# Layer 0's first norm: x projected un-normalized for three column blocks, then normalized in place by GpSimd

## The chip, the cores and the metric

One core of one Trainium2 chip. The metric is device time in microseconds (us) of one execution of the whole program, two layers of a hybrid model step. The engines are TensorE (PE), VectorE (DVE), ScalarE (ACT), GpSimd (POOL) and SyncE (SP, which here issues most DMAs).

## The reference, cut to what matters

The program runs 1024 prompt tokens and 32 sample tokens (8 sequences of 4) through two layers. What the change touches is how each layer begins:

```
def rmsnorm(x, g):                      # mean over the 1024 features of a token
    y = x * rsqrt(mean(x * x) + EPS)
    return y * g
h = rmsnorm(x, g_pre_mix[l])            # x: 1056 tokens x 1024
a_h, a_b, a_c, b_q, b_k, b_v, c_q, c_k, c_v, c_qi, c_ki, c_wi, d_u, d_v = split(h @ w_in[l])
# four mixers follow: a gated convolution, dilated attention, sparse attention with an
# indexer (c_qi, c_ki, c_wi) that picks 256 keys per query, and a gated spatial mix;
# then x += rmsnorm(m @ w_o), a feed-forward with its norms, and the next layer
```

Since `(x * r * g) @ W = r * (x @ (g * W))`, with `r` one number per token, the norm can be put before the projection, or its gain into the weights and its `r` behind the projection.

## The kernel before, in words

x lies transposed in SBUF, features on partitions: `xT` and `hT` are [128, 8, 1056] (8 chunks of 128 features, 1056 tokens). Tokens come in nine tiles of 128 (the last has the 32 sample tokens).

`load_x` is a block of its own, and a barrier of all engines ends it. SP loads the nine tiles of x as they are in HBM (512 KB each), then the gain `g`, the first two column blocks of `w_in` (`load_columns`), constants and the rope tables, and writes x to a parking place in HBM (`xpark`, three pieces). PE turns each tile with 8 transposes. DVE and ACT copy them out of PSUM into `xT`. ACT squares x, PE sums the squares over partitions with matmuls against ones, ACT takes the root, DVE inverts it and writes `hT`, the normalized x, for tokens 0 to 383. POOL starts 12 gathers of index pages.

`mix_in` projects. Its work is a list of units, each one token tile (or third) of one column block, in this order in layer 0: units 0 to 4 are block IX (the indexer's columns) of tiles 0 to 4; 5 to 7 are CV of tiles 0 to 2; 8 to 11 are IX of tiles 5 to 8; 12 to 17 are CV of the rest; 18 to 26 are CQ; 27 to 35 are CK; then DV, A0, A1, BQ, BK, BV, AB, DU. Two weight slots alternate by block. For each unit PE runs `project(i)`; ACT copies the result out (`unload`), DVE applies rope to the blocks that want it (`rotate`), and PE turns these four units later (`turn`), so unit 4 of PE stands behind the rope of unit 0, and unit 29 behind that of unit 25. All queues are written out by hand in unit order. A sample tile is projected in part beside the tile that `parts_at` names, and summed at the end of its block.

In layer 0 the rest of the norm is in `mix_in`: DVE's `second_norm` writes `hT` for tokens 384 to 767 before its first rope, and for the last 288 tokens ACT squares (`square_left`), PE sums (lines 876 and 881, at units 4 and 5), ACT takes the root, and DVE's `invert_left` and `norm_left` (lines 1352, 1358) write `hT` at unit 6. Layer 1 does the same for its last third, with a different source.

DVE waits ahead of its first rope for `in_`, six DMAs of constants, whose last is `own_col` (512 KB into `ext_p`), the first DMA that SP issues in `mix_in`. From unit 8 on, index scores are computed beside the projections (PE `index_heads`, ACT `index_relu`, DVE `index_scores`). At unit 24 DVE runs `search_begin`, which multiplies seven score tiles by a sign (line 1217) and then begins a bitwise search for each row's 256th score (line 1195 and the small operations of lines 1231, 1232, 1200) that goes on beside the projections to the end of `mix_in`.

The waits that matter: PE's `project` waits for `second_h` at unit 3 and for `left_h` from unit 8 on.

Of the kernel before, what the change touches and what calls it, by code (L numbers as in the profile page):

```python
# [6 lines left out]
ALU = mybir.AluOpType  # L7
# [8 lines left out]
P = 128  # L16
# [61 lines left out]
FIRST_LEFT, NEXT_LEFT = 6 * P, 2 * TH  # L78

FIRST_GATHERS = 12  # L80

ROOT_AT = 224000
# [160 lines left out]
def load_x(c, st):  # L243


    nc, io, ps, xT, hT = c.nc, c.io, c.ps, c.xT, c.hT
    PIECES = ((0, 3), (3, 6), (6, TILES))
    at = lambda p_: slice(PIECES[p_][0] * P, min(PIECES[p_][1] * P, T))
    wide = lambda p_: at(p_).stop - at(p_).start
    xt = nc.alloc_sbuf_tensor_at("x_tok", [P, TILES, D], F32, offset=c.m_at)  # L250
    W_SQ = 4
    sb = lambda n, shape, dt=F32: c.sb(n, shape, dt, stack=st)
    sb("x_tok_place", [P, 1024])
    page_step, places, tables = sb("page_step", [P, 1]), sb("places", [1, DB * PAGES]), sb("tables", [1, DB * PAGES], I32)
    g, sq, rstd = c.gains[:, 3, :], sb("first_sq", [P, W_SQ, 3 * P]), sb("first_rstd", [P, 3 * P])
# [3 lines left out]
    ident_in, table_in, g_in, rope_in, ones_set, placed, spread, rows_set, turned, kept_1, kept_2, squared, summed, rooted, inverted, h_done = (  # L259
        s(n) for n in ("ident_in", "table_in", "g_in", "rope_in", "ones_set", "placed", "spread", "rows_set", "turned", "kept_1", "kept_2", "squared",  # L260
                       "summed", "rooted", "inverted", "h_done"))
    NB_TURN = 6
    with nc.Block() as block:  # L263
        @block.sync
        def _(sp):
            sp.dma_start(tables[:, :], io["page_table"].rearrange("b p -> (b p)").rearrange("(o n) -> o n", o=1)).then_inc(table_in, 16)
            sp.dma_start(page_step[:, :], io["page_step"]).then_inc(table_in, 16)
            sp.dma_start(c.ident[:, :], io["ident"]).then_inc(ident_in, 16)
            for n in range(TILES):
                src = io["x_prompt"][0, n * P:n * P + P, :] if n < PT else io["x_sample"].rearrange("b t d -> (b t) d")  # L270
# [7 lines left out]
            for p_, (_, end) in enumerate(PIECES):  # L278
                sp.wait_ge(kept_1, end)
                sp.wait_ge(kept_2, end)  # L280
                sp.dma_start(c.xpark.rearrange("p (k t) -> p k t", k=KC)[:, :, at(p_)], xT[:, :, at(p_)]).then_inc(c.x_parked if p_ < 2 else c.x_last_parked, 16)
# [3 lines left out]
        @block.gpsimd  # L285
        def _(pool):
            pool.memset(c.ones[:, :], 1.0).then_inc(ones_set, 1)
            pool.memset(c.eps[:, :], EPS).then_inc(ones_set, 1)
            pool.wait_ge(rows_set, 4)
            for i in range(FIRST_GATHERS):  # L290
                gather_index_page(c, pool, i, c.page_rows)

        @block.tensor
        def _(pe):
            def turn(*tiles):
                for n in tiles:
                    m = tok(n)
                    pe.wait_ge(x_in[n], 16)
                    for half in range(2):
                        i = 2 * n + half  # L300
                        if i >= NB_TURN:
                            j = i - NB_TURN
                            pe.wait_ge(kept_2 if j % 2 else kept_1, j // 2 + 1)
                        for q in range(4):
                            k = 4 * half + q
                            ins = pe.transpose(ps[:, i % NB_TURN, q * P:q * P + m], xt[:m, n, k * P:(k + 1) * P], c.ident[:m, :m])
                        ins.then_inc(turned, 1)

            def total(p_):
                if p_:  # L310
                    pe.wait_ge(rooted, p_)
                for k in range(KC):
                    pe.wait_ge(squared, KC * p_ + k + 1)
                    pe.matmul(ps[:, 6, 0:wide(p_)], c.ones[:, :], sq[:, k % W_SQ, 0:wide(p_)], start=k == 0, stop=k == KC - 1).then_inc(summed, 1)

# [4 lines left out]
            turn(0, 1, 2, 3)  # L320
            total(0)
            turn(4, 5, 6)
            total(1)
            turn(7, 8)

        @block.scalar
        def _(act):
            def keep_first(n):
                act.wait_ge(turned, 2 * n + 1)
                act.activation(xT[:, 0:4, cols(n)], ps[:, 2 * n % NB_TURN, :].rearrange("p (k t) -> p k t", k=4)[:, :, 0:tok(n)],  # L330
                               ACT.Copy).then_inc(kept_1, 1)

            def keep(*tiles):
                for n in tiles:
                    act.wait_ge(turned, 2 * n + 2)
                    act.activation(xT[:, 4:8, cols(n)], ps[:, (2 * n + 1) % NB_TURN, :].rearrange("p (k t) -> p k t", k=4)[:, :, 0:tok(n)],
                                   ACT.Copy).then_inc(kept_2, 1)

            def square(p_):
                act.wait_ge(kept_1, PIECES[p_][1])  # L340
                act.wait_ge(kept_2, PIECES[p_][1])
                for k in range(KC):
                    if KC * p_ + k >= W_SQ:
                        act.wait_ge(summed, KC * p_ + k - W_SQ + 1)
# [2470 lines left out]
```

## Time and profile before

| | us |
|---|---|
| median of three runs | 3081.53 (3081.17 to 3081.68) |
| profiled execution, whole | 3083.07 |
| its span | 3081.5 |
| PE busy | 3010.2 (98%) |
| DVE busy | 1413.6 (46%) |
| ACT busy | 1054.3 (34%) |
| POOL busy | 739.2 (24%) |
| mean granted TensorE clock | 0.993 |

The span is the time from the first to the last recorded instruction; 1.6 us of the profiled execution lie around it. Times in the profile are counted from the span's start. Layer 0's `load_x` fills 0 to 29.3 us, its `mix_in` 29.3 to 430.8 us.

### The profile page before, as it was taken

How to read it: one execution, taken by the hardware profiler on the slowest of the kernel's cores; microseconds unless marked ns; L12 is line 12 of the kernel's file. 1: busy time of each engine (PE TensorE's matmuls, PEld its weight loads, DVE VectorE, ACT ScalarE, POOL GpSimd, SP SyncE). 2: the span in 40 equal slices, each digit the busy share in tenths (PEclk: the TensorE clock that was granted, in tenths of full speed). 3: DMA queues.
4: the chain of work that ended last, by engine and by line, in shares of the span. 5: the costliest groups of instructions: out<-in, count | busy, mean ns of one | idle time of the engine just before them, and what ended most of it. 6: DMA issues, size and time to landing. Idle time of an engine off the chain costs nothing. (4 is left out here: it accounts for less than half of the span.)

```text
span 3081.5 us, 48869 instructions
## 1 busy us (share of the span) xinstructions
PE 3010.2 (98%) x19766; PEld 2636.6 (86%) x19766; DVE 1413.6 (46%) x3342; ACT 1054.3 (34%) x2094; POOL 739.2 (24%) x526
## 2 busy tenths in 40 slices
PE   8999999999999999999999999999999999999998
PEld 6777766679999999999977777665899999999997
DVE  5579675467511111122565887654584111111125
ACT  4376535564311111011333665355642111110112
POOL 3002031324322122243300301312352122121131
PEclk9999999999999999999999999999999999999999
DMA  5120335651211111122321112457311111111131
GB/s 185 34 64 28 111 112 179 233 195 52 67 48 42 48 48 45 45 66 63 110 78 47 47 35 91 161 185 246 133 59 60 49 49 47 43 49 48 42 118 57
DMA packets 254071, 263.53 MB, mean 86 GB/s; under 512 B 24993, under 2 KB 224570, under 8 KB 253850
## 3 DMA queue, kind: packets, MB, share of 16 engines
q1 hardware_dynamic: 233370, 189.11, 19.5%
q0 software_dynamic: 20480, 71.32, 6.7%
q8 instruction: 158, 2.59, 0.3%
q14 instruction: 63, 0.52, 0.1%
HBM read 229.73 MB, written 30.65 MB: 84 GB/s over the span
## 5 line engine op out<-in xcount | busy, mean ns | idle before, releaser
L2230 PE MATMUL ps<-act_lo,w_hi 128*128 128x352 f32 x2112 | 683.5, 324 | 5.4 <-DVE act_lo L2683 3.8
L2230 PE MATMUL ps<-act_hi,w_hi 128*128 128x352 f32 x2112 | 677.1, 321 | 0.0
L2230 PE MATMUL ps<-act_hi,w_lo 128*128 128x352 f32 x2112 | 676.9, 321 | 0.0
L2604 POOL TENSOR_TENSOR w_lo<-w_raw,w_hi 128x1024 fp32r<-128x1024 f32 x132 | 324.4, 2460 | 1021.4 <-ACT w_hi L2444 1021.3
L740 PE MATMUL ps<-w_in_slots,hT 128*128 128x256 f32 (+1 forms) x2048 | 448.3, 375 | 3.1 <-PEq L263 1.7
L740 PEld LDWEIGHTS ps<-w_in_slots,hT 128*128 128x128 f32 x2048 | 374.3, 193 | 59.0 <-issue 12.6
L2230 PEld LDWEIGHTS ps<-act_lo,w_hi 128*128 128x128 f32 x2112 | 396.2, 188 | 11.1 <-DVE act_lo L2683 5.9
L2696 DVE TENSOR_TENSOR a_raw<-ps,silu 128x352 f32<-128x352 f32 x120 | 63.0, 525 | 728.6 <-PE ps L2230 728.5
L2230 PEld LDWEIGHTS ps<-act_hi,w_hi 128*128 128x128 f32 x2112 | 396.9, 188 | 0.2
L2230 PEld LDWEIGHTS ps<-act_hi,w_lo 128*128 128x128 f32 x2112 | 396.0, 187 | 0.0
L2230 PE MATMUL ps<-a_lo,w_hi 128*128 128x352 f32 x1056 | 343.9, 326 | 0.0
L2230 PE MATMUL ps<-a_hi,w_lo 128*128 128x352 f32 x1056 | 340.0, 322 | 0.0
L2230 PE MATMUL ps<-a_hi,w_hi 128*128 128x352 f32 x1056 | 339.7, 322 | 0.0
L2444 ACT ACTIVATE w_hi<-w_raw 128x1024 fp32r<-128x1024 f32 x132 | 139.7, 1058 | 457.6 <-DMA w_raw<-in_w_down 286.5
L2492 ACT ACTIVATE silu<-ps 128x352 f32<-128x352 f32 x120 | 55.8, 465 | 676.4 <-PE ps L2230 676.4
L743 PE MATMUL ps<-hT,w_in_slots 128*128 128x352 f32 x768 | 229.7, 460 | 0.0
L1195 DVE TENSOR_SCALAR_CACHE_REDUCE mask_c<-score,sel_cand 128x1024 bf16<-128x1024 f32 x248 | 219.1, 939 | 0.4
L743 PEld LDWEIGHTS ps<-hT,w_in_slots 128*128 128x128 f32 x768 | 145.1, 190 | 80.9 <-issue 1.6
L2230 PEld LDWEIGHTS ps<-a_lo,w_hi 128*128 128x128 f32 x1056 | 199.3, 189 | 1.1
L2230 PEld LDWEIGHTS ps<-a_hi,w_hi 128*128 128x128 f32 x1056 | 198.4, 188 | 1.1
L2230 PEld LDWEIGHTS ps<-a_hi,w_lo 128*128 128x128 f32 x1056 | 198.2, 188 | 0.0
L971 ACT ACTIVATE mask_s<-xT,sel_cand 32x2080 bf16<-32x2080 f32 x62 | 125.3, 2020 | 32.4 <-DVE sel_cand L1200 32.2
(368 smaller groups left out, 4245.2 us busy)
## 6 DMA issues: line engine op xcount, KB each, us to landing
w_raw<-in_w_gate SPq DMA_DIRECT2D x44, 512.0 KB, 3.7
w_raw<-in_w_up SPq DMA_DIRECT2D x44, 512.0 KB, 3.7
w_raw<-in_w_down SPq DMA_DIRECT2D x44, 512.0 KB, 3.7
w_in_slots<-in_w_in SPq DMA_DIRECT2D x18, 1024.0 KB, 5.2
xpark<-xT SPq DMA_DIRECT2D x9, 1408.0 KB, 5.6
xT<-xpark SPq DMA_DIRECT2D x6, 1408.0 KB, 14.5
hT<-xpark SPq DMA_DIRECT2D x6, 1408.0 KB, 12.9
wo_raw<-in_w_o SPq DMA_DIRECT2D x16, 512.0 KB, 5.3
```

The costliest lines, as they stand in the source:

```text
L740: ins = pe.matmul(ps[:m, bank[i], 0:w], hT[:, k, cols(n)], W[:, g % 2, k, 0:w], start=(k == 0), stop=(k == KC - 1))
L743: ins = pe.matmul(ps[:, bank[i], 0:TH], W[:, g % 2, k, n * P:(n + 1) * P], hT[:, k, th * TH:(th + 1) * TH], start=(k == 0), stop=(k == KC ...
L971: act.activation(junk[x], score[x], ACT.Sign, bias=cand[:rows[x], at[x]].bitcast(F32), accum_out=count[:rows[x], at[x]]).then_inc(q["count ...
L1195: return dve.tensor_scalar(junk[x], score[x], value, None, ALU.is_ge, ALU.add, accum_out=acc)
L2230: ins = pe.matmul(bank(b), w, x, start=first and i == 0, stop=end and i == 2)
L2444: act.activation(w_hi[slot(j)][:, 0:K, :], w_raw[slot(j)][:, 0:K, :], ACT.Copy).then_inc(w_hi_done, 1)
L2492: act.activation(sg(f, th), bank(unit_bank(n)), ACT.Silu).then_inc(sg_done, 1)
L2604: pool.tensor_tensor(w_lo[slot(j)][:, 0:K, :], w_raw[slot(j)][:, 0:K, :], w_hi[slot(j)][:, 0:K, :].bitcast(F32), ALU.subtract).then_inc(w_ ...
L2696: dve.tensor_tensor(raw, bank(unit_bank(n)), sg(chunk(p_, i), th), ALU.mult).then_inc(mul, 1)
```

## The change

In `load_x` nothing is summed over partitions any more. DVE alone copies the turned tiles, and straight into `hT`, un-normalized. ACT squares each tile as it came from HBM, tokens on partitions, with an accumulator that gives each token's sum of squares, and takes one root of [128, 9]. DVE multiplies the gain into the first weight block (`fold_gain`). SP issues `g` and the first weights after four tiles of x, the other five tiles behind them. POOL starts 9 gathers in place of 12. x is parked from `hT`.

In `mix_in` of layer 0, blocks IX, CV and CQ are projected from the un-normalized x with weights that hold the gain; ACT's `unload` multiplies by the token's inverse root. DVE's `first_columns` inverts the [128, 9] roots, spreads them over 1152 columns and folds the gain into CV's weights; POOL folds it into CQ's. PE turns the spread rows with nine transposes at unit 4, ACT keeps them as `first_rows`. `second_norm`, and in layer 0 `square_left`, both sums and `norm_left`, are gone. From unit 20 on POOL normalizes `hT` in place in three pieces of tokens (0 to 383, 384 to 767, 768 to 1055): per piece 8 times a `tensor_scalar` by the gain and a `tensor_tensor` by the rows, each waiting for the one before. A piece begins when IX, CV and CQ of its tiles are projected. PE's CK units (27 on) wait for the piece of their tile, and CK's sample part moves from unit 27 to unit 33. Layer 1 is as before.

```diff
 # load_x, SP
-            for n in range(TILES):
-                ...
-                sp.dma_start(xt[:tok(n), n, :], src).then_inc(x_in[n], 16)
+            load(0, 1, 2, 3)
             sp.dma_start(g, gain(io["g_pre_mix"], 0)).then_inc(g_in, 16)
             load_columns(c, sp, 0, 0)
+            load(4, 5, 6, 7, 8)
             load_columns(c, sp, 1, 0)
...
-                sp.wait_ge(kept_1, end)
-                sp.wait_ge(kept_2, end)
-                sp.dma_start(... xT[:, :, at(p_)]).then_inc(...)
+                sp.wait_ge(kept, 2 * end)
+                sp.dma_start(... hT[:, :, at(p_)]).then_inc(...)
 # load_x, ACT
+            for n in range(TILES):
+                ...
+                act.activation(sq[:m, :], xt[:m, n, :], ACT.Square, accum_out=c.first_sums[:m, n:n + 1]).then_inc(squared, 1)
+            act.wait_ge(squared, TILES)
+            act.activation(c.first_inv[:, :], c.first_sums[:, :], ACT.Sqrt, bias=c.eps[:, 0:1], scale=1.0 / D)
 # load_x, DVE
-            keep(0, 1, 2, 3, 4, 5)
-            first_h(0)
+            for i in range(2 * TILES):
+                n, half = divmod(i, 2)
+                dve.wait_ge(turned, i + 1)
+                dve.tensor_copy(hT[:, 4 * half:4 * half + 4, cols(n)], ...).then_inc(kept, 1)
+            dve.wait_ge(g_in, 16)
+            dve.wait_ge(c.w_in[0], 16)
+            fold_gain(c, dve, 0).then_inc(scaled, 1)
+def fold_gain(c, eng, g):
+    w = sum(x for _, x in BLOCKS[g])
+    W = c.W[:, g % 2, :, 0:w]
+    return eng.tensor_tensor(W, W, c.gains[:, 3, :].unsqueeze(2).to_broadcast([P, KC, w]), ALU.mult)
 # mix_in, PE
-                if l == 0 and i == 3:
-                    pe.wait_ge(second_h, KC)
-                if i >= T0 + T1:
+                if l == 0 and i == T0:
+                    pe.wait_ge(gain_folded, 1)
+                if l == 0 and i == first[CQ]:
+                    pe.wait_ge(queries_folded, 1)
+                if l == 0 and i >= first[CK]:
+                    pe.wait_ge(normed, KC * (n // 3 + 1) if g == CK else 3 * KC)
+                if l and i >= T0 + T1:
                     pe.wait_ge(left_h, KC)
...
+                if l == 0 and i == NORM_AT:
+                    pe.wait_ge(rows_spread, 1)
+                    for n in range(TILES):
+                        m = tok(n)
+                        ins = pe.transpose(ps[:, 5 + n // 3, n % 3 * P:n % 3 * P + m], spread_rows[:m, n, :], c.ident[:m, :m])
+                    ins.then_inc(rows_turned, 1)
 # mix_in, ACT unload
+                    if by_tokens(g):
+                        act.wait_ge(inv_set, 1)
+                        act.activation(dst, src[:, 0:w], ACT.Copy, scale=c.first_inv[:m, n:n + 1]).then_inc(freed_act, 1)
+                        return
 # mix_in, POOL
                     gather_index_page(c, pool, i, c.page_rows)
+                    if i == FIRST_GATHERS + 16:
+                        pool.wait_ge(w_in[CQ % 2], loads[CQ])
+                        fold_gain(c, pool, CQ).then_inc(queries_folded, 1)
+                pool.wait_ge(rows_kept, 2)
+                for p_, (a, e) in enumerate(FIRST_PIECES):
+                    ...
+                    pool.wait_ge(proj_done, max(i for i, (g, n, _) in enumerate(units) if g in (IX, CV, CQ) and n < e) + 1)
+                    for k in range(KC):
+                        pool.tensor_scalar(hT[:, k, at_p], hT[:, k, at_p], g_x[:, k:k + 1], None, ALU.mult).then_inc(first_scaled, 1)
+                        pool.wait_ge(first_scaled, KC * p_ + k + 1)
+                        pool.tensor_tensor(hT[:, k, at_p], hT[:, k, at_p], c.first_rows[:, at_p], ALU.mult).then_inc(normed, 1)
 # mix_in, DVE
-                second_norm()
+                first_columns()
+            def first_columns():
+                dve.reciprocal(c.first_inv[:, :], c.first_inv[:, :]).then_inc(inv_set, 1)
+                dve.wait_ge(inv_set, 1)
+                dve.tensor_copy(spread_rows, c.first_inv[:, :].unsqueeze(2).to_broadcast([P, TILES, P])).then_inc(rows_spread, 1)
+                dve.wait_ge(w_in[CV % 2], loads[CV])
+                fold_gain(c, dve, CV).then_inc(gain_folded, 1)
```

## Rows read from the trace of the kernel before

**Rows 1.** The page: busy time, share and instructions of each engine.

```profile
PE 3010.2 (98%) x19766; PEld 2636.6 (86%) x19766; DVE 1413.6 (46%) x3342; ACT 1054.3 (34%) x2094; POOL 739.2 (24%) x526
```

**Rows 2.** Timeline of PE, 25 to 50 us: start, duration, work [idle before <- releaser].

```profile
25.93 1.65 PE L306 MATMUL ps<-ident,x_tok 128*128 128x128 f32 x16
...
29.30 10.80 PE L740 MATMUL ps<-w_in_slots,hT 128*128 128x164 f32 x64 [1.72 <-PEq L263]
...
41.10 0.33 PE L760 MATMUL ps<-ident,stage 128*128 128x128 f32 x1 [1.01 <-DVE wi L1130]
...
43.70 1.18 PE L876 MATMUL ps<-hT,ones 128*32 128x288 f32 x16
...
48.54 0.65 PE L881 MATMUL ps<-left_part,ones 128*128 128x288 f32 x2
```

**Rows 3.** Timeline of DVE, its first wait for a constant in `mix_in`.

```profile
39.81 0.23 DVE L1380 CAST mask_c<-causal 128x128 bf16<-128x128 f32 x1 [3.57 <-DMA ext_p<-in_own_col]
```

**Rows 4.** Timeline of SP, the issue of CQ's weights in `mix_in`.

```profile
74.13 0.43 SPq L457 DMA_DIRECT2D w_in_slots<-in_w_in  x1
```

**Rows 5.** Windows: PE, PEld, DVE, ACT, POOL busy (x), PEclk, DMA share, GB/s.

```profile
30.00:32.00 2.00, 2.00 (x9) 2.00 (x9) 1.96 (x2) 0.00 (x0) 0.00 (x0) 0.50 1.06 388
...
38.00:40.00 2.00, 2.00 (x16) 1.84 (x14) 0.19 (x1) 1.21 (x4) 0.96 (x1) 1.00 0.27 86
40.00:42.00 2.00, 0.99 (x8) 0.90 (x8) 1.76 (x15) 0.73 (x3) 1.33 (x2) 1.00 0.01 2
```

**Rows 6.** Timeline of PE, units 20, 23, 27, 29 and 33.

```profile
112.75 3.62 PE L740 MATMUL ps<-w_in_slots,hT 128*128 128x256 f32 x16
...
135.02 3.62 PE L740 MATMUL ps<-w_in_slots,hT 128*128 128x256 f32 x16
...
149.04 1.07 PE L732 MATMUL ps<-w_in_slots,hT 128*32 128x256 f32 x16
...
157.27 0.38 PE L760 MATMUL ps<-ident,stage 128*128 128x128 f32 x2
...
172.40 3.62 PE L740 MATMUL ps<-w_in_slots,hT 128*128 128x256 f32 x16
```

**Rows 7.** POOL's instructions by line and shape: xcount | busy, mean ns | idle before.

```profile
L1068 POOL TENSOR_SCALAR vn<-vn,ln_mv,ln_r 128x256 f32<-128x256 f32 x16 | 19.3, 1214 | 373.3 <-DVE ln_r L1400 373.3
...
L1090 POOL TENSOR_TENSOR xT<-xT,mask_s 32x2080 f32<-32x2080 f32 x2 | 8.2, 4114 | 101.9 <-DVE xT L1267 101.9
...
L1090 POOL TENSOR_TENSOR score<-score,mask_c 128x384 f32<-128x384 f32 x2 | 1.8, 918 | 4.4 <-DVE score L1267 4.4
```

**Rows 8.** The chain that ended last: two POOL operations, each waiting for the other.

```profile
3004.86 0.96 POOL down_acc L2647
3005.95 0.96 POOL down_acc L2647
```

**Rows 9.** DVE's instructions by line, 148.6 to 153.8 us.

```profile
L1217 DVE TENSOR_SCALAR score<-score,sel_sign 128x1024 f32<-128x1024 f32 (+5 forms) x6 | 3.5, 587 | 0.2
L1217 DVE TENSOR_SCALAR xT<-xT,sel_sign 32x2080 f32<-32x2080 f32 x1 | 1.3, 1291 | 0.0
```

**Rows 10.** Timeline of DVE: `rotate` of unit 25, and operations beside busy POOL.

```profile
154.77 0.23 DVE L1121 TENSOR_TENSOR stage<-rope 128x64 f32<-128x64 f32 x1
...
230.88 0.29 DVE L1231 TENSOR_TENSOR sel_ok<-sel_count,sel_bound 128x7 int32<-128x7 f32 x1 [0.22 <-ACT mask_c L971]
...
240.45 9.75 DVE L1231 TENSOR_TENSOR sel_ok<-sel_count,sel_bound 128x7 int32<-128x7 f32 x1
...
391.01 2.96 DVE L1264 TENSOR_SCALAR ki_in<-score,sel_bound 128x1024 bf16<-128x1024 f32 x1
```

**Rows 11.** Timeline of POOL beside those DVE operations.

```profile
226.98 10.87 POOL L1068 TENSOR_SCALAR vn<-vn,ln_mv,ln_r 128x256 f32<-128x256 f32 x9 [139.34 <-DVE ln_r L1400]
237.83 6.19 POOL L1073 TENSOR_TENSOR vn<-vn,ki_in 128x256 f32<-128x256 f32 x9
...
389.30 4.11 POOL L1090 TENSOR_TENSOR xT<-xT,mask_s 32x2080 f32<-32x2080 f32 x1 [50.96 <-DVE xT L1267]
```

More of the change, by code:

```diff
@@ L258, in load_x @@
     x_in = [s(f"in{n}") for n in range(TILES)]
-    ident_in, table_in, g_in, rope_in, ones_set, placed, spread, rows_set, turned, kept_1, kept_2, squared, summed, rooted, inverted, h_done = (
-        s(n) for n in ("ident_in", "table_in", "g_in", "rope_in", "ones_set", "placed", "spread", "rows_set", "turned", "kept_1", "kept_2", "squared",
-                       "summed", "rooted", "inverted", "h_done"))
+    ident_in, table_in, g_in, rope_in, ones_set, placed, spread, rows_set, sums_set, turned, kept, squared, scaled = (
+        s(n) for n in ("ident_in", "table_in", "g_in", "rope_in", "ones_set", "placed", "spread", "rows_set", "sums_set", "turned", "kept",
+                       "squared", "scaled"))
     NB_TURN = 6
@@ L294, in _ @@
         def _(pe):
[L295 to L314, printed above, removed]
             pe.wait_ge(ones_set, 2)
@@ L319, in _ @@
             pe.wait_ge(ident_in, 16)
[L320 to L324, printed above, removed]
+            for i in range(2 * TILES):
+                n, half = divmod(i, 2)
+                m = tok(n)
+                if half == 0:
+                    pe.wait_ge(x_in[n], 16)
+                if i >= NB_TURN:
+                    pe.wait_ge(kept, i - NB_TURN + 1)
+                for q in range(4):
+                    k = 4 * half + q
+                    ins = pe.transpose(ps[:, i % NB_TURN, q * P:q * P + m], xt[:m, n, k * P:(k + 1) * P], c.ident[:m, :m])
+                ins.then_inc(turned, 1)
@@ L326, in _ @@
         @block.scalar
         def _(act):
[L328 to L344, printed above, removed]
-                    act.activation(sq[:, k % W_SQ, 0:wide(p_)], xT[:, k, at(p_)], ACT.Square).then_inc(squared, 1)
-            def root(p_):
-                act.wait_ge(summed, KC * p_ + KC)
-                act.activation(c.first_root[:, :] if p_ else rstd[:, :], ps[:, 6, 0:wide(p_)], ACT.Sqrt, bias=c.eps[:, 0:1], scale=1.0 / D).then_inc(rooted, 1)
@@ L623, in mix_in @@
         done_by[i] = sum(e <= due for e in ends)
-    left = slice(NEXT_LEFT if l else FIRST_LEFT, T)
+    left = slice(NEXT_LEFT, T)
     wide = left.stop - left.start
-    assert T0 * P <= FIRST_LEFT and T0 * P <= NEXT_LEFT
+    assert T0 * P <= NEXT_LEFT
     NORM_AT = T0 - 1
-    second = slice(3 * P, 6 * P)
     g_y, g_x, rstd_y, rstd_x = c.gains[:, 2, :], c.gains[:, 3, :], c.rstd_y[:, 0:wide], c.rstd_x[:, 0:wide]
@@ L1359, in norm_left @@
                                              op0=ALU.mult, op1=ALU.mult).then_inc(left_h, 1)
-            def second_norm():
-                dve.reciprocal(c.first_root[:, :], c.first_root[:, :]).then_inc(second_inv, 1)
-                dve.wait_ge(second_inv, 1)
-                for k in range(KC):
-                    dve.scalar_tensor_tensor(out=hT[:, k, second], in0=c.xT[:, k, second], scalar=g_x[:, k:k + 1], in1=c.first_root[:, :],
-                                             op0=ALU.mult, op1=ALU.mult).then_inc(second_h, 1)
+            def first_columns():
[4 more added lines that the diff above has]
+                fold_gain(c, dve, CV).then_inc(gain_folded, 1)
             if l:
```

100 lines of the change are left out of this document (52 added, 48 removed).

## The prediction

> **What bounds the kernel now.** I read the page first: PE is busy 98% of the span [rows 1], so a change pays only where it ends an idle stretch of PE or takes work from it, and costs wherever PE is made to wait. Then I read PE's timeline over layer 0's beginning [rows 2]. The reader is to see one idle stretch of 1.72 us between the last turned tile and the first projection (the barrier that ends `load_x`), another of 1.01 us ahead of unit 4, whose releaser is DVE's rope (line 1130), and the sums of lines 876 and 881. DVE's timeline says why that rope was late: DVE waited 3.57 us, to 39.81, for a constant, `own_col` [rows 3]. The windows say why the constant was late: at 30 to 32 us the DMA engines moved 388 GB/s at a full share, at 38 to 40 their share fell to 0.27, at 40 to 42 to 0.01 [rows 5]. `own_col` is the last thing in a queue that was never empty. So DMA sets when unit 4 starts, not the norm. From unit 4 on PE is nearly gapless to the end of `mix_in`. Last I read what the new POOL work will meet: PE's units 20 to 33 [rows 6], POOL's prices [rows 7, 8] and how POOL and DVE get on [rows 9 to 11].
>
> **Front of layer 0.** The change takes work from PE, ACT and DVE in `load_x`: the sums and `first_h`, and in `mix_in` `second_norm`, which lies before DVE's wait for `own_col` [rows 3] and so is hidden already. The barrier may come 1 to 2 us earlier, since only transposes at the pace of x and the parking issues are left. But everything that stood in the DMA queue ahead of `own_col` still stands there: the same x, weights, constants and three parkings. Only gathers of 64 KB fall behind it, 12 against 9 of them in `load_x`, and those of `mix_in` come back in part. At the 388 GB/s of [rows 5] one is 0.17 us; I take one to three, -0.2 us. Unit 4 then starts at about 40.9 us where it starts at 41.10. The earlier start of units 0 to 3 turns into a longer idle stretch in front of unit 4: their 10.80 us would begin at 27 to 28.3 and end at 38 to 39, and PE would stand for 1.8 to 3 us. That has a price. After 1.72 us idle the clock was granted at 0.50, that is 1.2 GHz, in the window from 30 us; after 1.01 us it stayed at 1.00, 2.4 GHz, in that of 40 to 42 [rows 5]. The four cold-started units took 10.80 us, while one warm unit of this size took 2.39 us in the same timeline, so 9.56 for four: a fall costs 1.2 us. I take it whole; bounds 0 (no fall) and 2.4 (one unit of 2.39 us at half speed).
>
> PE's own work at units 4 and 5: line 876 was busy 1.18 us and line 881 0.65, of which some 0.2 overlap their neighbours as a matmul's end does, so 1.6 us go. Nine transposes come; sixteen took 1.65 us [rows 2], so 0.9 us. Net -0.7 us. DVE's inverse, spread and fold of CV lie in its wait for `own_col`; were that cover gone, the fold alone, which has as many columns as CQ's, could cost up to the 4.1 us worked out for that one below. ACT's scaled copies cost what its plain ones do, as far as I can tell, and nobody waits for them.
>
> POOL's fold of CQ is a TENSOR_TENSOR of 2048 elements per partition. 2080 took 4.11 us and 384 took 0.92 [rows 7], that is 0.19 us and 1.88 ns per element, so 4.1 us. The weights are issued at 74.13 [rows 4], so it runs from about 79, where DVE computes index scores from two SBUF inputs and PE waits for the ACT copies behind them. Such a DVE operation can be shut out by POOL: 7 columns took 9.75 us at 240.45, as long as POOL's back-to-back TENSOR_TENSORs lasted, and 0.29 us beside POOL's TENSOR_SCALARs [rows 10, 11]. PE meets only what is left of it behind DVE and ACT and their idle time, so I let 0.5 of the 4.1 us reach it; bounds 0 and 4.1. POOL's 16th-and-later gathers stand behind the fold, and are wanted only 30 us later. Front in all: -0.2 - 0.7 + 1.2 + 0.5 = +0.8 us.
>
> **Normalizing in place.** Pairs of TENSOR_SCALAR and TENSOR_TENSOR. The second, of 384 columns, is 0.92 us, of 288 columns 0.74. The first has one row near it: two operations on 256 columns took 1.21 us [rows 7]. With one operation for two I halve what is over 0.19 us: 0.70, or 2.0 ns per element, so 0.96 at 384 and 0.76 at 288. From below it can't be under one pass at half of that, 0.6; from above it may cost as the two do, 4.0 ns per element, 1.73 and 1.34. A wait for the operation before costs 0.13 us (1.09 from start to start, 0.96 busy [rows 8]). A piece of 384: 8 x (0.96 + 0.92 + 0.13) = 16.1 us; the last piece: 8 x (0.76 + 0.74 + 0.13) = 13.0 us.
>
> Piece 0 starts when unit 20 ends, 116.4, and ends at 132.5; unit 27 wants it at 149: hidden (at the upper price 138.6, still hidden). Piece 1 starts when unit 23 ends, 138.6. Pieces 1 and 2 need 29.1 us, to 167.7. Unit 33 starts at 172.40 and, as the sample part leaves unit 27 (1.0 us [rows 6]), now at 171.4. So on paper 3.7 us are over. But DVE's `search_begin` falls into that time: seven TENSOR_SCALARs of line 1217, 4.8 us [rows 9]. That POOL and such an operation don't run together is in the trace: line 1264 took 2.96 us at 391.01 while POOL's 4.11 us operation ran from 389.30 to 393.41, and ended at 393.97, 0.56 us behind it, about the 0.59 of line 1217 [rows 9 to 11]. POOL thus loses 4.8 us and about 1 us to rope: to 173.5, a stall of 2.1 us at unit 33.
>
> DVE loses too. Its seven operations alternate with POOL's of 0.94 us on average: if only TENSOR_TENSOR shuts them out three waits, if both kinds do seven, so 2.8 to 6.6 us. The rope of unit 25 behind them ended at 155.0 [rows 10]; PE wants it for its turn at 157.27 less 1.0 [rows 6]. Slack is 1.3 us, the stall 1.5 to 5.3; middle 3.4. While PE stands POOL goes on, so of 3.4 and 2.1 us the larger counts. From then on PE is gapless again and what is late stays late: DVE and ACT have more room when PE is later.
>
> The Trainium skill, page "SBUF — State Buffer", section "SBUF: two separate sides", says that the port pair which GpSimd shares with VectorE is locked for a whole instruction, not shared, both against a VectorE operation in a two-port mode and against one with two SBUF inputs. The 2.96 us and the 9.75 us agree with it. By that rule all seven operations alternate with both kinds, which is the 5.3 us end; the 0.29 us beside TENSOR_SCALAR doesn't show a full instruction's wait, so I stay at the middle.
>
> **Sum.** Front +0.8, stall +3.4, together +4.2 us. Profiled execution 3083.07 + 4.2 = 3087.3, of which span 3085.7. The median of the runs is 3081.53, 1.5 us below the profiled execution, and the same sum gives 3085.7. This is 0.14% slower; 0.2% (6.2 us) is about what a measurement of this kernel can tell from no change.
>
> **Rivals.**
> - POOL is late for good. If one operation costs what two do, pieces 1 and 2 take 8 x (1.73 + 0.92 + 0.13) + 8 x (1.34 + 0.74 + 0.13) = 39.9 us, with DVE's 5.8 to 184.3, a stall of 12.9 us at unit 33: with the front +13.7, median 3095.2. For it: the only row of the kind [rows 7]. Against it: half the arithmetic. It decides from 1.2 us per 384-column TENSOR_SCALAR on.
> - POOL is in time and DVE doesn't feel it: TENSOR_SCALAR at 0.6 us and only rare shut-outs. No stall, the front alone, -1.0 to +1.5: 3081.8. For it: the 0.29 us beside POOL's TENSOR_SCALAR [rows 10, 11]. The Trainium skill, page "GPSIMD Engine Reference", section "Engine selection", says that one-input operations run at roughly line rate there; no one-operation TENSOR_SCALAR is in this trace, and its 1.21 us for two speaks against it as a rule.
> - The front gain arrives, and the end is faster. If `own_col` lands a microsecond or more before 39.8, because the 16 DMA engines empty earlier when parking is issued earlier, unit 4 keeps the lead: the 1.0 us of the barrier, the 1.01 us of idle, 0.7 of sums: -2.7, median 3078.8, provided there is no stall later. It decides once the constant lands before 39 us. Against it: the full DMA share up to 38 us.
> - The change doesn't do what it says: the barrier stays at 29.3, as parking can't be issued earlier. It changes nothing in the sum, as unit 4 is set by `own_col`.
>
> **Chances.** Forecast case (+1.5 to +6.2) 0.40; POOL late (over +6.2) 0.25; hidden (-1 to +1.5) 0.20; front gain (below -1) 0.15. Range: from 3079.5, inside the front gain's case, to 3093.5, which leaves out the upper end of POOL late: together about 0.2. The forecast case's own range is 3083.0 to 3087.7. Faster by over 0.2% would need -6.2 us, more than the front holds: 0.02. Slower by over 0.2%: 0.27. Within: 0.71.
>
> **What would show it.** Right: `own_col` still ends DVE's wait at 39 to 40 us and unit 4 starts near 40.9, with a longer idle stretch before it and a half-clock stretch behind it; POOL's pairs take 2.0 us; line 1217's operations are 1 to 2 us each; PE waits for DVE's rope at unit 29, 2 to 5 us, or for POOL's `hT` at unit 33. Wrong: a `tensor_scalar` of 1.7 us or of 0.6; line 1217 unchanged at 0.59; unit 4 before 40 us; or a new idle stretch of PE elsewhere, such as unit 3 to 17 for lack of a folded weight.

## The result, and the profile after

| | before | after |
|---|---|---|
| median, 14 runs of each | 3081.12 | 3086.7 |
| span of the profiled execution | 3081.5 | 3087.2 |
| mean granted TensorE clock | 0.993 | 0.991 |

One of the 14 runs after is in a slow state (4640.37 us at a clock of 0.601); the ratio leaves it out, and without it the median after is 3086.05 us.

The ratio is 1.0018, 95% interval 1.001 to 1.0026: by it 5.5 us slower, where 4.2 were forecast. Both profiled executions lie 2 to 3 us above these medians (3083.07 and 3088.99 us), so what a single trace shows need not be the size in the median run. The page after, busy times of the engines, against [rows 1]:

```profile
PE 3006.8 (97%) x19725; PEld 2636.7 (85%) x19725; DVE 1420.2 (46%) x3331; ACT 1050.8 (34%) x2075; POOL 791.4 (26%) x576
```

TensorE has 3.4 us less work, GpSimd 52 us more, and the end is later. Where that happens is read from TensorE's timeline. First the front, against [rows 2]:

```profile
26.82 11.55 PE L708 MATMUL ps<-w_in_slots,hT 128*128 128x164 f32 x64 [3.93 <-PEq L261]
...
40.34 0.33 PE L728 MATMUL ps<-ident,stage 128*128 128x128 f32 x1 [1.97 <-DVE wi L1128]
40.61 2.39 PE L708 MATMUL ps<-w_in_slots,hT 128*128 128x164 f32 x16
```

The first projection starts 2.5 us earlier, is slower (11.55 against 10.80 us; the clock is at 0.50 in the windows from 26 to 30 us and 0.57 in the next), and ends in a longer wait for VectorE's rope at unit 4. VectorE's wait for `own_col`, against [rows 3], and TensorE's window at unit 4, against [rows 5]:

```profile
39.05 0.23 DVE L1378 CAST mask_c<-causal 128x128 bf16<-128x128 f32 x1 [8.39 <-DMA ext_p<-in_own_col]
```

```profile
40.00:42.00 2.00, 1.66 (x12) 1.66 (x13) 1.69 (x12) 0.45 (x2) 0.85 (x1) 1.00 0.31 74
```

`own_col` comes 0.76 us earlier, unit 4 by as much, and unit 4's 16 matmuls take 2.39 us: no clock fall behind 1.97 us of standing. The sums of lines 876 and 881 gone against nine transposes give the rest, 0.5 us: at the sample part of CQ TensorE is 1.3 us ahead of before (98.87 against 100.14), and still is at unit 28.

Then TensorE's timeline over units 27 to 33, against [rows 6]:

```profile
147.77 3.62 PE L708 MATMUL ps<-w_in_slots,hT 128*128 128x256 f32 x16
...
151.44 3.62 PE L708 MATMUL ps<-w_in_slots,hT 128*128 128x256 f32 x16
158.73 0.69 PE L728 MATMUL ps<-ident,stage 128*128 128x128 f32 x2 [3.67 <-DVE stage L1119]
159.21 6.40 PE L708 MATMUL ps<-w_in_slots,hT 128*128 128x256 f32 x16
165.55 0.31 PE L728 MATMUL ps<-ident,stage 32*128 32x32 f32 x2
...
177.00 1.07 PE L700 MATMUL ps<-w_in_slots,hT 128*32 128x256 f32 x16
```

This is the whole loss. Ahead of unit 29 TensorE stands 3.67 us for the rope of unit 25 (`stage`, written by line 1119 on VectorE), and unit 29, which takes 3.62 us elsewhere, takes 6.40. From the start of unit 28 to that of unit 30 TensorE needs 14.35 us where it needed 7.47; these 6.9 us less the lead of 1.3 are the 5.6 us by which unit 33's matmuls are late (178.00 against 172.40). The windows of the same time, with the granted clock as the third number from the right:

```profile
156.00:158.00 2.00, 0.00 (x0) 0.00 (x0) 1.73 (x7) 0.00 (x0) 1.92 (x3) 1.00 0.00 0
158.00:160.00 2.00, 1.27 (x4) 1.16 (x5) 1.83 (x7) 0.39 (x1) 1.92 (x3) 0.50 0.03 10
160.00:162.00 2.00, 2.00 (x6) 1.57 (x5) 1.76 (x6) 0.00 (x0) 1.92 (x3) 0.50 0.62 128
162.00:164.00 2.00, 2.00 (x6) 1.55 (x6) 0.60 (x4) 0.00 (x0) 1.92 (x3) 0.50 0.59 161
164.00:166.00 2.00, 2.00 (x9) 1.42 (x8) 0.00 (x0) 0.35 (x2) 1.92 (x3) 0.79 0.52 95
```

TensorE was idle from 155.1 to 158.7, and from 158 to 164 it got 1.2 GHz instead of 2.4; half as many matmuls (x6) fit a window. From unit 33 on (177.00 with the 1.07 us of the sample part ahead, before 172.40 without it) the distance stays at 5.6 to 5.7 us to the end. Layer 0's attention and all that follows are the same.

Why the rope was late, VectorE's timeline, against [rows 9, 10]:

```profile
148.23 0.90 DVE L1213 TENSOR_TENSOR sel_exact<-sel_exact,count_bounds 128x7 f32<-128x7 f32 x1
149.16 3.67 DVE L1215 TENSOR_SCALAR score<-score,sel_sign 128x1024 f32<-128x1024 f32 x4
152.87 1.51 DVE L1215 TENSOR_SCALAR xT<-xT,sel_sign 32x2080 f32<-32x2080 f32 x1
154.41 2.03 DVE L1215 TENSOR_SCALAR score<-score,sel_sign 128x768 f32<-128x768 f32 x2
...
157.06 0.91 DVE L1115 TENSOR_TENSOR rope<-stage,rope_h 128x64 f32<-128x64 f32 x1
...
158.45 0.23 DVE L1119 TENSOR_TENSOR stage<-rope 128x64 f32<-128x64 f32 x1
```

From the last compare of the sample scores (144.71) to the end of the rope VectorE needs 14.0 us, where it needed 9.9. The seven multiplications by the signs take 7.1 us for 4.8 (the six of `score` 926 ns each for 587); a 7-column operation takes 0.90 for 0.17; the rope 1.6 for 0.7. And GpSimd's side, its instructions by line and shape (xcount | busy, mean ns | idle before):

```profile
L1059 POOL TENSOR_SCALAR hT<-hT,gains 128x384 f32<-128x384 f32 x16 | 20.7, 1292 | 23.3 <-PE ps L708 23.3
L1061 POOL TENSOR_TENSOR hT<-hT,first_rows 128x384 f32<-128x384 f32 x16 | 17.2, 1072 | 1.3
L1059 POOL TENSOR_SCALAR hT<-hT,gains 128x288 f32<-128x288 f32 x8 | 8.0, 1004 | 0.0
L1061 POOL TENSOR_TENSOR hT<-hT,first_rows 128x288 f32<-128x288 f32 x8 | 6.4, 795 | 0.7
```

Undisturbed, a pair of 384 columns goes 2.31 us from start to start (1.25 and 1.00 busy). The last piece ended at 172.8, in time for unit 33 at 177.00.

### The profile page after: what moved, and what is told of

Its sections match the earlier page's. It is cut to its first block and busy times, and to the rows that moved or that the text cites. A ratio compares the mean times of both kernels' runs of the same rounds, so it can differ in the third digit from the quotient of the medians.

```text
span 3087.2 us, 48819 instructions
## 1 busy us (share of the span) xinstructions
PE 3006.8 (97%) x19725; PEld 2636.7 (85%) x19725; DVE 1420.2 (46%) x3331; ACT 1050.8 (34%) x2075; POOL 791.4 (26%) x576
```

## The experiments

Each group ran on one chip beside the kernel before. On the chips of the first four and of the last run, everything took some 25 to 29 us longer (the kernel before 3106.87 and 3110.14 us), so ratios are compared within a group, and across groups with care. The changed kernel itself was run on the chips of the first result and of the second group alone.

**First group: the kernel before had a median of 3106.87 us.**

`e1_rope_first`: after, with `search_begin` one unit later, behind the rope of unit 25.

```diff
                 if k == HC + 2:
                     sample_keep(HC)
+                if k == HC + 2 + (l == 0):
                     search_begin()
```

> The changed kernel, but in layer 0 DVE runs search_begin one unit later, behind the rope of unit 25. Theory 1 (PE waits at unit 29 for that rope, since search_begin is stretched by POOL's work): the rope of unit 25 ends near 148 us in place of 158.7, the 3.67 us wait and the clock's fall behind it (2.8 us) go, 6.5 us in all; POOL's last piece still ends near 172.8, while unit 33 now comes at about 170.2, so a wait of up to 2.6 us for hT takes its place. Net -4 us against the changed kernel, about -1.5 us against the kernel before. Rival (GpSimd's normalization is late by itself and the rope's wait only hides it): PE waits as long for hT, and the time stays within 1 us of the changed kernel's.

Measured: 3108.07 us, ratio 1.0001 (0.9992 to 1.001). The changed kernel was not run on this chip, so the time can't decide between the two. The wait at unit 29 is gone, none for `hT` has come in its place, and TensorE waits at unit 30 for the next rope, TensorE's timeline:

```profile
163.62 0.31 PE L728 MATMUL ps<-ident,stage 32*128 32x32 f32 x2 [2.33 <-DVE stage L1119]
163.86 5.41 PE L708 MATMUL ps<-w_in_slots,hT 128*128 128x256 f32 x16
```

`search_begin` as a whole is too long for a single place: behind the rope of unit 25 it makes that of unit 26 late by 2.33 us, and the clock falls behind it again.

`e2_before_with_pool_load`: the kernel before, with 24 pairs of the same two operations of GpSimd on an unused part of `mT`, nothing else changed. Here the `tensor_scalar` too waits for the operation before it, so a pair of 384 columns goes 2.43 us from start to start where it goes 2.31 in the change.

```diff
                     gather_index_page(c, pool, i, c.page_rows)
+                for last, w in ((20, 384), (23, 384), (26, 288)):
+                    pool.wait_ge(proj_done, last + 1)
+                    ...
+                        pool.tensor_scalar(x, x, g_x[:, k:k + 1], None, ALU.mult)
+                        pool.tensor_tensor(x, x, ones, ALU.mult)
```

> The kernel before, and beside it GpSimd does the changed kernel's 24 pairs of tensor_scalar and tensor_tensor, of the same widths and at the same units, on a scratch row that nobody reads; its output is unchanged. Theory 1 (contention of POOL and DVE alone makes the loss): search_begin's seven multiplications take about 7.2 us in place of 4.8, the rope of unit 25 ends some 5 us late, its slack here is 2.3 us, so PE waits 2.5 to 3 us at unit 29, and up to 2.8 us more if the clock falls: +2.6 to +5.4 us against the kernel before. Rival (the loss comes from another part of the change, the folded weights, the scaled copies or the wait for hT): within 0.5 us of the kernel before.

Measured: 3107.18 us, ratio 1.0005 (0.9995 to 1.0014), 0.3 us above the kernel before, where theory 1 had 2.6 to 5.4: by the time, the rival's case. The trace tells more. VectorE's multiplications by the signs, grouped, and TensorE at unit 29:

```profile
L1230 DVE TENSOR_SCALAR score<-score,sel_sign 128x1024 f32<-128x1024 f32 (+5 forms) x6 | 4.8, 800 | 0.2
L1230 DVE TENSOR_SCALAR xT<-xT,sel_sign 32x2080 f32<-32x2080 f32 x1 | 1.9, 1928 | 0.0
```

```profile
162.63 0.44 PE L761 MATMUL ps<-ident,stage 128*128 128x128 f32 x2 [1.22 <-DVE stage L1134]
162.90 3.62 PE L741 MATMUL ps<-w_in_slots,hT 128*128 128x256 f32 x16
```

587 ns have become 800, and a wait at unit 29 appears in a kernel that had none [rows 6]. GpSimd's load alone makes it; nothing else of the change is in this kernel. But the load alone gives only a third of the wait of 3.67 us, no fall of the clock, and no loss that the time shows. TensorE stands 1.22 us only, because TensorE is further behind there: from VectorE's compare of the sample scores to the end of unit 28 this kernel has 12.3 us, after has 10.4 (1.0 of it is the sample part that the change moved, the rest TensorE's lead), and VectorE needs 13.5 us here and 14.0 in after from that compare to the end of the rope (9.9 in before).

`e3_own_col_early` and `e4_before_own_col_early`: `own_col` loaded with `load_x`'s constants into a place of its own, on after and on before.

```diff
             load_index_constants(c, sp)
+            sp.dma_start(c.own_first[:, :], io["own_col"]).then_inc(c.const_in, 16)
...
-            sp.dma_start(late_e[:, 1024:2048], io["own_col"]).then_inc(in_, 16)
             if l:
+                sp.dma_start(late_e[:, 1024:2048], io["own_col"]).then_inc(in_, 16)
```

> The changed kernel, but in layer 0 the constant own_col is loaded in load_x, ahead of the rope tables and of the three parkings of x, into the same place. Theory 1 (own_col behind the parkings sets when unit 4 starts): DVE's 8.4 us wait goes, unit 4 starts behind unit 3 at about 38.4 us in place of 40.34, and all that follows is 1.9 us earlier: 1.9 us less than the changed kernel. Rival (the DMA queue as a whole sets it, by x_parked or by w_in): unit 4 starts where it does, the time is the changed kernel's.

> The kernel before with the same move of own_col. Theory 1: the 1.01 us wait ahead of unit 4 goes and nothing else changes, -1.0 us against the kernel before. Rival: no change, since the rope tables and parkings behind own_col are later by its 1.3 us and the barrier that ends load_x with them.

Measured: 3103.05 us, ratio 0.9989 (0.998 to 0.9998) on after; 3108.69 us, ratio 1.0006 (0.9997 to 1.0015) on before. In both the wait at unit 4 is gone. The 1.9 us that e3 was to gain on the changed kernel can't be read off, as that did not run here; e3 is 5.0 us faster than e1, in which unit 4 has a wait of 2.70 us and takes 4.07. The 1.0 us of e4 isn't seen. On after the wait at unit 29 stays at 3.64 us. On this chip the kernels with the old `load_x` had their first projection at 35 to 36 us, those with the new one at 27 to 28, TensorE's timeline of e4 and of e3:

```profile
25.12 6.79 PE L316 MATMUL ps<-first_sq,ones 128*128 128x384 f32 x16 [3.24 <-ACT first_sq L347]
...
35.12 2.19 PE L744 MATMUL ps<-w_in_slots,hT 128*128 128x164 f32 x14 [1.73 <-PEq L264]
```

```profile
27.82 11.43 PE L712 MATMUL ps<-w_in_slots,hT 128*128 128x164 f32 x64 [5.52 <-PEq L262]
39.31 2.39 PE L712 MATMUL ps<-w_in_slots,hT 128*128 128x164 f32 x16
```

So the front of the kernel before is some 6 us longer there than in [rows 2], with TensorE waiting for the squares, and the change's is not. What makes it longer on that chip was not found.

**Second group: the kernel before had a median of 3081.2 us.**

`e5_after_again`: the changed kernel as it is.

> The changed kernel as it is, to stand beside the experiments that edit it. On the chip of the first four experiments the kernel before took 3106.9 us, some 25 more than on the chip of the first result, and the kernels that begin as the one before does showed their first projection at 35 to 36 us, not 29.3. Theory A, that the 5.6 us lie in units 4 to 33 whatever the chip: ratio to the kernel before 1.0018, as first measured. Theory B, that the norm by tokens needs x less early and so gains where x comes late: the first projection stays at 27 to 28 us, and the ratio falls below 1.001; profile: a wait of 3.6 to 3.7 us of TensorE ahead of unit 29 in either.

Measured: 3087.53 us, ratio 1.002 (1.0011 to 1.0029), theory A's number. Two rows differ from the first trace of the same kernel:

```profile
40.87 0.33 PE L728 MATMUL ps<-ident,stage 128*128 128x128 f32 x1 [2.98 <-DVE wi L1128]
...
41.14 4.07 PE L708 MATMUL ps<-w_in_slots,hT 128*128 128x164 f32 x16
...
160.97 0.69 PE L728 MATMUL ps<-ident,stage 128*128 128x128 f32 x2 [3.64 <-DVE stage L1119]
161.44 4.99 PE L708 MATMUL ps<-w_in_slots,hT 128*128 128x256 f32 x16
```

`own_col` landed half a microsecond later, the wait at unit 4 was 2.98 us instead of 1.97, and now the clock did fall there (4.07 us for unit 4, not 2.39). The fall at unit 29 cost 1.4 us here, not 2.8; the clock is 0.70, 0.50 and 0.95 in the windows from 160 to 166 us, where after has 0.50 three times and 0.79 from 158 to 166.

`e6_signs_between_ropes`: after, the seven multiplications in three groups behind the ropes of units 25, 26 and 27.

```diff
-                for x in SLOTS:
-                    step(dve.tensor_scalar(score[x], score[x], sign[...], None, ALU.mult))
...
+                if l == 0 and k in (HC + 3, HC + 4, HC + 5):
+                    search_signs((SLOTS[0:3], SLOTS[3:5], SLOTS[5:7])[k - HC - 3])
```

> After, with the seven multiplications by the signs in three groups (3, 2, 2) behind the ropes of units 25, 26 and 27, in place of all seven ahead of the rope of unit 25. Theory A (VectorE, slowed by GpSimd, is late for the rope of unit 25, and the clock falls in that wait): the waits of 3.67 us at unit 29 and of 2.3 us at unit 30 (seen with the whole search_begin behind the rope) are both gone, no stretch between 155 and 170 us has a clock of 0.50, and the kernel is 6.0 to 6.5 us faster than after, ratio to after 0.998. Rival (GpSimd itself is late for good, and VectorE's wait only covered it): TensorE now waits for GpSimd's second third at unit 30 or its last at unit 33, 3 us or more, and less than 3 us are gained.

Measured: 3086.57 us, ratio 1.0015 (1.0006 to 1.0024), 1 us less than e5, which is within the noise. VectorE is in time for every rope, and TensorE waits for GpSimd:

```profile
175.67 1.94 PE L700 MATMUL ps<-w_in_slots,hT 128*32 128x256 f32 x16 [2.90 <-POOL hT L1061]
177.53 4.67 PE L708 MATMUL ps<-w_in_slots,hT 128*128 128x256 f32 x11
```

The rival was right. The last piece is late by 2.90 us at unit 33, and the clock falls behind this wait in place of the other (1.94 us for the sample part, not 1.07, and 5.74 for the whole of unit 33, not 3.72). In after that lateness was covered by the wait at unit 29.

`e7_both`: the edit of e6 and `own_col` with the constants.

> The edit of e6_signs_between_ropes and own_col loaded with the constants. Own_col early gave about 4 us beside the kernel before's runs (3103.05 against 3106.87) with the wait at unit 29 still there. Theory A: the two gains add, some 6 us below e3's, ratio to the kernel before 0.997. Rival (GpSimd late for good): the front is 2 us earlier and GpSimd's last third, which starts when the second is done, is not, so that TensorE waits 1 to 3 us at unit 33 and the ratio is 0.998 to 0.999.

Measured: 3081.51 us, ratio 1.0003 (0.9993 to 1.0012). Against e6 in the same group 5.1 us less: the 2.93 us of waiting at unit 4 and the 1.7 us of its fall account for 4.6. (Between the two traces it is more, 6.6 us at unit 33: e6 has a fall of the clock near 72 us too, worth 1.6, which e7 has not. See the last section.) The two gains of theory A don't both come: the wait for GpSimd at unit 33 is 2.91 us as in e6, since GpSimd's pieces start behind TensorE's units and move with them. The rival's "last third does not move" was wrong in that, but its wait is there.

`e8_unit_28_twice`: after, with unit 28's matmuls issued twice.

```diff
-                    for k in range(KC):
+                    for k in 2 * tuple(range(KC)) if l == 0 and i == 28 else range(KC):
```

> After, with the 16 matmuls of unit 28 (3.45 us) issued twice into the same bank, so that TensorE works through most of the wait of 3.67 us instead of standing. The second pass writes the same values. Theory A (the clock falls because TensorE stands, and 2.85 us of the loss is this fall): 16 more matmuls and yet 2.5 to 3 us faster than after; the windows of 158 to 166 us are at 1.00 and unit 29 takes 3.6 us in place of 6.4. Rival (the slow unit comes of something else, the DMA traffic or GpSimd's load at that time): unit 29 still takes 6.4 us and the time is that of after within 0.5 us.

Measured: 3085.73 us, 1.8 us less than e5 beside it, with 3.45 us of matmuls more:

```profile
151.61 7.07 PE L708 MATMUL ps<-w_in_slots,hT 128*128 128x256 f32 x32
158.87 0.44 PE L728 MATMUL ps<-ident,stage 128*128 128x128 f32 x2 [0.19 <-DVE stage L1119]
159.15 3.62 PE L708 MATMUL ps<-w_in_slots,hT 128*128 128x256 f32 x16
```

TensorE stood 0.19 us, every window from 150 to 172 us had a clock of 1.00, and unit 29 took 3.62 us. DMA traffic (127, 155 and 90 GB/s in the windows from 160 us, in after 128, 161 and 95) and GpSimd's load (1.92 of 2 us) are there as in after, so it is the standing that the slow unit follows. This rests on the trace, which is that of the fastest of the 11 runs (3082.46 us); the 1.8 us between the medians are at the edge of the noise. The gain is less than the 2.5 to 3 us expected: the fall doesn't cost the 2.8 us of the first trace in every execution (in e5's it cost 1.4).

**Third group: the kernel before had a median of 3080.39 us.**

`e9_two_scalars`: GpSimd's operation with the rows replaced by a second multiplication by the gain. The kernel leaves the inverse root out of CK and what follows.

```diff
-                        pool.tensor_tensor(hT[:, k, at_p], hT[:, k, at_p], c.first_rows[:, at_p], ALU.mult).then_inc(normed, 1)
+                        pool.tensor_scalar(hT[:, k, at_p], hT[:, k, at_p], g_x[:, k:k + 1], None, ALU.mult).then_inc(normed, 1)
```

> After, with GpSimd's multiplication of hT by the row of inverse roots (tensor_tensor, 1.00 us at 384 columns) replaced by a second multiplication by the gain (tensor_scalar, 1.25 us at 384); the inverse root is left out of the projections of CK and later. GpSimd is then busy with tensor_scalar alone. Theory A (it is the two-input operation that shuts VectorE out, and tensor_scalar only a little): the seven multiplications by the signs take 4.9 to 5.5 us in sum, not 7.2, no VectorE operation of 32 to 64 columns takes 0.8 us or more between 148 and 165 us, and the wait at unit 29 is 1 us or less. Rival (any GpSimd work shuts it out): the seven take 7.2 us or more and the wait is 3.7 us. In either, GpSimd needs 2.66 us per pair in place of 2.31, so that TensorE waits for it at unit 30 or 33.

Measured, in a single execution: 3086.87 us. VectorE's seven multiplications, grouped, and TensorE at units 29 and 33:

```profile
L1215 DVE TENSOR_SCALAR score<-score,sel_sign 128x1024 f32<-128x1024 f32 (+5 forms) x6 | 4.7, 776 | 0.2
L1215 DVE TENSOR_SCALAR xT<-xT,sel_sign 32x2080 f32<-32x2080 f32 x1 | 1.5, 1491 | 0.0
```

```profile
155.93 0.44 PE L728 MATMUL ps<-ident,stage 128*128 128x128 f32 x2 [0.81 <-DVE stage L1119]
...
176.65 1.94 PE L700 MATMUL ps<-w_in_slots,hT 128*32 128x256 f32 x16 [5.37 <-POOL hT L1061]
```

Most of theory A: the wait at unit 29 is 0.81 us, the 7-column operation back at 0.17 us, the rope at 0.7, and no small VectorE operation there is over 0.56. Not as expected: the seven still take 6.2 us, not 4.9 to 5.5. So `tensor_scalar` alone stretches them (776 ns for 587), beside both kinds they are stretched more (926), and it takes GpSimd's two-input kind to hold VectorE's short operations up for 0.8 us or more.

`e10_gain_on_scalar`: after, the last piece's gain multiplied by ScalarE.

```diff
+                if l == 0 and i == first[CQ] + PT:
+                    ...
+                    for k in range(KC):
+                        act.activation(hT[:, k, 6 * P:T], hT[:, k, 6 * P:T], ACT.Copy, scale=g_x[:, k:k + 1]).then_inc(last_scaled, 1)
...
+                        if p_ < 2:
                             pool.tensor_scalar(hT[:, k, at_p], hT[:, k, at_p], g_x[:, k:k + 1], None, ALU.mult).then_inc(first_scaled, 1)
```

> After, with the gain of the last third (8 multiplications of 288 columns) done by ScalarE behind its eviction of unit 26, in place of GpSimd. e6 and e7 showed GpSimd late by 2.9 us at unit 33 as soon as VectorE was in time. Theory A (two waits in parallel, of which either alone costs about the same): the wait of 3.7 us at unit 29 stays, since GpSimd's work of that time is the second third's, GpSimd ends some 8 us earlier, at 165 us, and the time is that of after within 0.05 %, ratio to the kernel before 1.0015 to 1.002. Rival (VectorE's wait came mostly of the last third): the wait at unit 29 shrinks under 2 us and 3 us are gained.

Measured: 3089.15 us, ratio 1.0026 (1.0015 to 1.0037). It is above after's 1.0018 and 1.002, but not clear of them, as the intervals overlap; that nothing is gained is theory A's. Neither theory had the longer wait of the trace. GpSimd does end at 165.8. But its two-input operations now follow each other with nothing between, and each of the four steps of the rope of unit 25 waits for one; GpSimd's and VectorE's timelines:

```profile
158.79 7.00 POOL L1068 TENSOR_TENSOR hT<-hT,first_rows 128x384 f32<-128x384 f32 x9
```

```profile
158.98 0.91 DVE L1122 TENSOR_TENSOR rope<-stage,rope_h 128x64 f32<-128x64 f32 x1
159.81 0.79 DVE L1123 TENSOR_TENSOR rope<-stage,rope_h 128x32 f32<-128x32 f32 x1
160.53 0.82 DVE L1124 TENSOR_TENSOR rope<-stage,rope_h 128x32 f32<-128x32 f32 x1
161.38 0.75 DVE L1126 TENSOR_TENSOR stage<-rope 128x64 f32<-128x64 f32 x1
```

3.15 us for a rope of 0.69, and the wait at unit 29 grows from 3.67 to 5.18 us.

`e11_all`: the edits of e6, e7 and e10 together.

> After with all three edits: signs between the ropes, own_col with the constants, the last third's gain on ScalarE. Theory A: the wait of 2.9 us at unit 33, the last one seen between units 4 and 33, is gone, so the kernel is 2.5 to 3.5 us faster than e7's 3081.5 and about 3 us faster than the kernel before, ratio 0.999. Rival (a third engine is late next: ScalarE, held 3 us by the eight multiplications, is late with the stages of units 27 and 28): a wait of 1 us or more at unit 31 or 32, ratio 0.9997 or more.

Measured: 3076.84 us, ratio 0.9987 (0.9978 to 0.9996), faster than both kernels. Between units 4 and 33 no wait of 1 us or more is left but two for ScalarE, of 1.88 us at 68 and 1.73 us at 97, which before and after have too. TensorE at unit 33, GpSimd's last operations ended at 163.4:

```profile
169.09 1.07 PE L705 MATMUL ps<-w_in_slots,hT 128*32 128x256 f32 x16
```

**Alone: the kernel before had a median of 3110.14 us.**

`e12_all_but_own_col`: e11 with `own_col` where the change loads it.

> e11_all without its edit of own_col: own_col is loaded where the change loads it, so that TensorE stands at unit 4 as in the changed kernel (1.97 to 2.98 us in its executions so far, followed in those of 2.9 us and more by a slower unit 4, 4.07 us in place of 2.39). Theory A (the two late engines cost what the change lost, and the front by itself is a small gain): no wait of 1 us or more between units 5 and 33; 2 to 4 us above e11 beside the same kernel before, ratio to the kernel before 0.9995 to 1.0005, that is the change with its losses around units 29 and 33 taken away and nothing else gained. Rival (own_col early made no difference and e11's gain came of the other two alone): ratio 0.9985 to 0.999.

Measured: 3105.47 us, ratio 0.9986 (0.9977 to 0.9995). Between units 5 and 33 there is no wait of 1 us or more but those two for ScalarE; at unit 4 TensorE stands 3.54 us and the unit takes 4.58. The rival's ratio came, but it can't be taken for the rival: this is a slow chip again, where the old front was the longer one in e2 and e4, and e6 against e7 has shown on a single chip that `own_col` early is worth 5 us beside the signs moved. That the change without its two late engines is faster than the kernel before is shown for this chip only.

## Why the prediction was nearly right, point by point

**The mechanism was right.** The loss is a wait of TensorE ahead of unit 29 for the rope of unit 25, behind multiplications by signs that GpSimd slowed. Forecast 3.4 us, measured 3.67. e2 made a wait there by GpSimd's load alone (1.22 us), e9 took most of it away by changing one of GpSimd's two operations, e6 took it away by moving VectorE's work. That the size fits so well is in part luck: VectorE lost 4.1 us, not the 4.7 of the middle, and the slack was 0.4 us, not 1.3. TensorE came for the rope at 155.06 with the front's whole lead of 1.3, VectorE had only 0.4 of it, and undisturbed (9.9 us from 144.71) would have been done at 154.6.

**Both sides late, the larger counts.** Forecast: 2.1 us for GpSimd at unit 33 beneath VectorE's. e6 and e7 measured 2.90 and 2.91 once VectorE was in time. That is why removing the visible wait alone gave 1 us.

**The step that failed: after the stall "PE is gapless again".** The prediction priced a fall of the clock at unit 4, and none at unit 29, where TensorE was to stand longer. In the first trace it was the other way round: none at unit 4, 2.8 us at unit 29 (6.40 for 3.62). Unit 4 is not safe, either: e5, the same kernel, has 1.7 us there. So the term belonged to both places, at 0 to 1.7 and 1.4 to 2.8 us by the two traces of this kernel. Nor was the kernel before free of it between units 4 and 33: its clock falls behind the wait of 1.88 us at 70 us (last section).

**The front was mis-sized, -1.3 us for +0.8.** `own_col` came 0.76 us earlier, not 0.2; the fall of 1.2 us didn't come; the 0.5 us for the fold of CQ didn't reach TensorE; and the sums gave 0.5 us, not 0.7. The fold took 3.60 us (forecast 4.1), three of VectorE's index scores beside it 5.77 us for 2.46, but TensorE's lead of 1.3 us is whole at unit 28. These 2.1 us and the missing fall of 2.8 have opposite signs; that the sum is off by only 1.5 us in the spans (+5.7 against +4.2) is partly luck.

**GpSimd's price was too low, its disturbance too high.** 1.25 and 1.00 us for the `tensor_scalar` of 384 and 288 columns, forecast 0.96 and 0.76, and 2.31 us for a pair of 384, forecast 2.01. That is beyond the 1.2 us from which the rival "POOL is late for good" was to decide, and yet it isn't late by 12.9 us: the rival took 5.8 us of lost time beside VectorE, and the second piece took 20.3 us instead of 18.5 (8 times 2.31), a loss of 1.8. The last piece ended at 172.8, forecast 173.5: two errors that nearly cancel.

**By the skill's rule.** The Trainium skill, page "SBUF — State Buffer", section "SBUF: two separate sides", has both kinds of VectorE operations shut out for whole instructions. e9 doesn't bear this out: beside `tensor_scalar` alone the seven multiplications lose 1.3 us in all, about one of GpSimd's operations (1.25 us), not one each. For the short two-input ones GpSimd's two-input operation does cost a whole instruction (0.90 us for 0.17, 3.15 us for the rope in e10), as the page has it; beside its `tensor_scalar` e9 has them at 0.17 to 0.56 us. The measurement decides. The page "GPSIMD Engine Reference", section "Engine selection", of the Trainium skill has one-input operations at roughly line rate; here 384 columns cost GpSimd 1.25 us with one input and 1.00 with two, and VectorE 0.42 with one (line 1217 of the kernel before), so the measurement differs.

## What to carry to other kernels

Work put on GpSimd is not free because GpSimd is idle: ask which VectorE operation runs at that time, and who waits for it; beside back-to-back two-input operations of GpSimd, a chain of short two-input operations such as a rope pays one whole GpSimd operation per step (3.15 us for 0.69 in e10). When a stall is removed, look at what it was covering: two late engines of about the same lateness cost only the larger. Here the fix of either alone gained 1 us or nothing (e6, e10); with both the wait is gone, and e11 is 5 us below e7, from which only the second fix is missing (1.0003 and 0.9987, on different chips). Price an idle stretch of TensorE at its length and what the clock may take behind it.

## What the runs showed of the hardware that was not expected

How much follows a wait of TensorE is not a fixed sum. Waits in layer 0's `mix_in`, and the unit behind them:

| wait, us | where | unit behind it, us (at full clock) |
|---|---|---|
| 0.81, 1.22 | e9 and e2, unit 29 | 3.62, 3.62 (3.62) |
| 1.69, 1.97, 1.98 | e9, after and e8, unit 4 | 2.39, 2.39, 2.39 (2.39) |
| 2.33 | e1, turn of unit 26 | 5.41 (3.72) |
| 2.70, 2.93, 2.97, 2.98, 3.54 | e1, e6, e10, e5 and e12, unit 4 | 4.07, 4.07, 4.02, 4.07, 4.58 (2.39) |
| 2.90, 2.91, 5.37 | e6, e7 and e9, sample part and unit 33 | 1.94 and 5.74, 1.07 and 3.72, 1.94 and 5.84 (1.07 and 3.72) |
| 3.64, 3.64, 3.67 | e3, e5, after, unit 29 | 4.85, 4.99, 6.40 (3.62) |
| 5.18 | e10, unit 29 | 5.79 (3.62) |

Of the waits over 2.3 us all but one (e7) were followed by a slower unit. Shorter ones are not safe: every trace has the same wait of 1.88 us for ScalarE ahead of unit 12, and in nine of the fourteen, before and after among them, the clock falls to 0.50 behind it; in e2, e3, e4, e7 and e12 it does not. The kernel before, and e4:

```profile
70.00 0.66 PE L770 MATMUL ps<-xT 32*128 32x128 f32 x8 [1.88 <-ACT vn L958]
...
71.20 1.94 PE L732 MATMUL ps<-w_in_slots,hT 128*32 128x256 f32 x16
```

```profile
73.31 0.50 PE L774 MATMUL ps<-xT 32*128 32x128 f32 x8 [1.88 <-ACT vn L962]
...
74.11 1.07 PE L736 MATMUL ps<-w_in_slots,hT 128*32 128x256 f32 x16
```

From there to the next such wait TensorE needs 29.0 to 29.2 us with the fall and 27.5 without, so it costs some 1.5. In the same way the first four units, behind the 1.7 us of the barrier, take 10.80 us in before, 10.82 in e2 and 9.52 in e4. What decides between a fall and none after the same wait, and between 4.85 and 6.40, isn't settled; a difference of 1.5 to 3 us between two single traces can come of this alone.
